# Seven block products in place of eight for part of gate and up in a two-layer decoder trunk

## The reference

```python
h2 = _rmsnorm(x, ffn_norm[l])
ff = jax.nn.silu(jnp.einsum('bsd,df->bsf', h2, w_gate[l])) * jnp.einsum('bsd,df->bsf', h2, w_up[l])
x = x + jnp.einsum('bsf,fd->bsd', ff, w_down[l])
```

## Time and profile before

| what | us |
| --- | --- |
| median of 3 runs | 2231.94 (2230.34 to 2232.48) |
| the profiled execution, its own time | 2232.38 |
| its span | 2230.6 |
| TensorE busy | 2212.5 |
| VectorE busy | 1277.2 |
| ScalarE busy | 948.6 |
| GpSimd busy | 24.0 |
| one pass of the feed-forward loop | 66.2 |

### The profile page before, as it was taken

One profiled execution on the slowest core, in us unless ns is written; L12 is line 12 of the kernel. 1 busy time (PEld: TensorE's weight loads), 2 busy tenths in 40 slices (PEclk: granted clock), 3 DMA queues, 4 the chain that ended last, 5 costly groups with the idle time before them and its releaser, 6 DMA issues.

```text
span 2230.6 us, 27421 instructions
## 1 busy us (share of the span) xinstructions
PE 2212.5 (99%) x11060; PEld 1889.3 (85%) x11060; DVE 1277.2 (57%) x1372; ACT 948.6 (43%) x964; POOL 24.0 (1%) x24
## 2 busy tenths in 40 slices
PE   9999999999999999999999999999999999999998
PEld 7899988888888888888888999888888888888886
DVE  5576774555455555555655866745555455555555
ACT  5554544533333333333443635444333333333333
POOL 0000000000000000000000000000000000000000
PEclk9999999999999999999999999999999999999999
DMA  7543455555555555555555435555555555555554
GB/s 249 183 134 117 157 170 189 182 191 192 189 188 188 188 190 190 192 190 192 193 179 160 147 114 166 174 171 189 197 190 192 190 189 188 188 190 189 192 191 160
DMA packets 221094, 402.67 MB, mean 181 GB/s; under 512 B 13376, under 2 KB 53600, under 8 KB 220896
## 3 DMA queue, kind: packets, MB, share of 16 engines
q1 hardware_dynamic: 220304, 400.90, 54.9%
q10 hardware_dynamic: 720, 0.78, 0.1%
HBM read 399.54 MB, written 2.10 MB: 180 GB/s over the span
## 4 chain that ended last, share of the span: by engine, by line
PE 97%; DMA 1%; DVE 1%; issue 1%; ACT 0%; SPq 0%; POOLq 0%; POOL 0%; ACTq 0%; DVEq 0%
PE bank L631 29%; PE bank L633 29%; PE bank L632 29%; PE bank L591 2%; DMA stage<-in_w_in 1%; PE bank L756 1%; PE bank L985 0%; PE bank L983 0%; PE bank L984 0%; PE bank L697 0%; PE bank L820 0%; PE bank L808 0%; PE bank L698 0%; PE bank L699 0%; PE bank L707 0%
## 5 line engine op out<-in xcount | busy, mean ns | idle before, releaser
L1332 DVE TENSOR_TENSOR w_lo<-stage,w_hi 128x2048 fp32r<-128x2048 f32 (+4 forms) x397 | 859.3, 2166 | 710.5 <-ACT w_hi L1022 710.4
L1022 ACT ACTIVATE w_hi<-stage 128x2048 fp32r<-128x2048 f32 (+4 forms) x397 | 719.8, 1815 | 957.7 <-DMA stage<-in_w_down 308.7
L631 PE MATMUL bank<-w_hi,xt_hi 128*128 128x512 f32 (+4 forms) x2328 | 876.6, 377 | 6.4 <-DVE xt_lo L1393 4.3
L633 PE MATMUL bank<-w_hi,xt_lo 128*128 128x512 f32 (+4 forms) x2328 | 867.7, 373 | 0.0
L632 PE MATMUL bank<-w_lo,xt_hi 128*128 128x512 f32 (+4 forms) x2328 | 867.0, 372 | 0.0
L631 PEld LDWEIGHTS bank<-w_hi,xt_hi 128*128 128x128 f32 x2328 | 437.7, 188 | 80.0 <-issue 11.8
L633 PEld LDWEIGHTS bank<-w_hi,xt_lo 128*128 128x128 f32 x2328 | 437.5, 188 | 69.0
L632 PEld LDWEIGHTS bank<-w_lo,xt_hi 128*128 128x128 f32 x2328 | 437.9, 188 | 67.8
L631 PE MATMUL bank<-w_hi,f_hi 128*128 128x512 f32 x640 | 249.1, 389 | 0.0
L633 PE MATMUL bank<-w_hi,f_lo 128*128 128x512 f32 x640 | 249.0, 389 | 0.0
L632 PE MATMUL bank<-w_lo,f_hi 128*128 128x512 f32 x640 | 249.0, 389 | 0.0
(11 more groups left out here) (213 smaller groups left out, 1231.9 us busy)
## 6 DMA issues: line engine op xcount, KB each, us to landing
stage<-in_w_gate SPq DMA_DIRECT2D x176, 512.0 KB, 4.3
stage<-in_w_up SPq DMA_DIRECT2D x176, 512.0 KB, 4.4
stage<-in_w_down SPq DMA_DIRECT2D x174, 512.0 KB, 4.4
stage<-in_w_in SPq DMA_DIRECT2D x96, 384.0 KB, 3.7
stage<-in_w_out SPq DMA_DIRECT2D x64, 512.0 KB, 4.4
stage<-in_w_in SPq DMA_DIRECT2D x54, 512.0 KB, 4.6
stage<-in_w_in SPq DMA_DIRECT2D x16, 320.0 KB, 3.4
stage<-in_w_q_b SPq DMA_DIRECT2D x12, 384.0 KB, 3.6
```

Of the source, the lines that this page charges most:

```text
L631: pe.matmul(acc, a, wh[:, i, :], start=first and i == 0, stop=False)
L633: mm = pe.matmul(acc, b, wh[:, i, :], start=False, stop=last and i == len(kts) - 1)
L1022: act.activation(w_hi[s][:, 0:kts * cols], stage[s][:, 0:kts * cols], ACT.Copy).then_inc(hi_made[s], 1)
L1332: vec.tensor_tensor(w_lo[s][:, 0:kts * cols], stage[s][:, 0:kts * cols], w_hi[s][:, 0:kts * cols].bitcast(F32), ALU.subtract).then_inc(lo_ ...
```

## The change

In chunks 2 to 10 the first 6 of the 16 row tiles are computed by a scheme of Strassen's kind (Winograd's form). Two token tiles, row tiles q and q+3, and the columns of gate and up form 2x2 blocks. The plain way takes 8 block products; here 7 products of sums of blocks (four sums of token blocks, made once a layer; three sums of weight blocks besides one overwritten block, made for each unit) do, and are combined afterwards. Three units (0, 2 and 4 of a chunk: "sets") hold one such set each, the five others (1, 3, 5, 6, 7: "pairs") hold two row tiles of gate and two of up and are computed plainly. Chunks 0 and 1 stay as they were; chunk 1 now stands ahead of the loop, with the down projection of chunk 0 behind it. The loop runs over chunks 2 to 9. All eight banks are used within a chunk: 0 to 3 for what belongs to one result each, 4 to 7 for products that several results share. `ff_turn` moves from inside gate and up to behind the down units, into banks 4 and 6.

PE (`product` is the three matmuls of a block):

```diff
+SETS = (0, 2, 4)
+PAIRS = (1, 3, 5, 6, 7)
+DOWN_BANKS = (4, 6), (5, 7), (4, 6), (5, 7)
+TURN_BANKS = (4, 6), (0, 1)
...
+                def set_unit(n, q, f, turn):
...
+                    if first:
+                        pe.wait_ge(act_made, layer * (FF_CHUNKS * NT) + NT * f)
+                        pe.wait_ge(xs_made, layer + 1)
+                    product(0, token(0, q), raw[0], first, False)
+                    product(1, mixed_x[3], raw[2], first, False)
+                    product(2, token(1, q), summed[2], first, False)
+                    if first:
+                        added(f - 2, 8)
+                    product(7, mixed_x[0], summed[1], first, last)
+                    product(5, mixed_x[2], summed[0], first, last)
+                    if first:
+                        hidden_in(f - 1)
+                    product(4, token(0, q + K_SET), raw[1], first, last)
+                    product(6, mixed_x[1], raw[3], first, last).then_inc(used[s], 1)
...
                     if c == 0:
-                        for b in (6, 7):
-                            pe.wait_ge(bank_free[b], ROUND[layer, ("ff_turn", 0)][b] + f + 2)
-                        added(f - 1, 6)
-                    elif c == 2:
-                        added(f, 2)
+                        hidden_in(f)
+                        if after_set:
+                            pe.wait_ge(first_kept, layer * SET_CHUNKS + f + 2 - FIRST_SET)
+                            pe.wait_ge(combined, layer * (2 * SET_CHUNKS) + 2 * (f + 1 - FIRST_SET) + 1)
+                    elif c == 1:
+                        if after_set:
+                            pe.wait_ge(combined, layer * (2 * SET_CHUNKS) + 2 * (f + 1 - FIRST_SET) + 2)
                     else:
-                        pe.wait_ge(silu_made if c == 1 else act_made, layer * (FF_CHUNKS * NT) + NT * (f + 2))
+                        added(f, 2 * c - 2)
...
+                with pe.Fori(FIRST_SET, FF_CHUNKS - 1) as f:
+                    gate_up_sets(f, U_BODY, 3 * f - 3 * FIRST_SET)
                     for c in range(4):
-                        down(f - 1, c, U_BODY + 8, 3 * f - 3)
+                        down(f - 1, c, U_BODY + 8, 3 * f - 3 * FIRST_SET)
+                    added(f - 1, 6)
+                    ff_turn(f, TURN_BANKS[0])
```

ACT, preparing a set unit, and DVE, preparing it and in its order around the down units:

```diff
+                    act.activation(w_hi[s][:, 0:3 * NCH], stage[s][:, 0:3 * NCH], ACT.Copy).then_inc(raw_hi_made, 1)
+                    if between:
+                        between()
+                    act.wait_ge(sums_made, layer * (K_SET * SET_CHUNKS) + set_index(n) + 1 + sets)
+                    act.activation(w_hi[s][:, 3 * NCH:], stage[s][:, 3 * NCH:], ACT.Copy)
+                    act.activation(sums_hi[s // 2][:, :, :], sums[s // 2][:, :, :], ACT.Copy).then_inc(hi_made[s], 1)
...
+                    vec.wait_ge(full[s], made(quad, n) * 32)
+                    vec.tensor_tensor(x[:, 0:2, :], w[:, 1:3, :], w[:, 3:4, :].to_broadcast([P, 2, NCH]), ALU.add)\
+                       .then_inc(sum_chain, 1)
+                    vec.wait_ge(sum_chain, 2 * k + 1)
+                    vec.tensor_tensor(w[:, 3, :], x[:, 0, :], w[:, 2, :], ALU.add).then_inc(sum_chain, 1)
+                    vec.wait_ge(sum_chain, 2 * k + 2)
+                    vec.tensor_tensor(x[:, 2, :], w[:, 3, :], w[:, 0, :], ALU.add).then_inc(sums_made, 1)
+                    if between:
+                        between()
+                    vec.wait_ge(sums_made, k + 1)
+                    vec.wait_ge(raw_hi_made, k + 1)
+                    vec.tensor_tensor(w_lo[s][:, 0:3 * NCH], stage[s][:, 0:3 * NCH], w_hi[s][:, 0:3 * NCH].bitcast(F32),
+                                      ALU.subtract)
+                    vec.wait_ge(hi_made[s], made(quad, n))
+                    vec.tensor_tensor(w_lo[s][:, 3 * NCH:], stage[s][:, 3 * NCH:], w_hi[s][:, 3 * NCH:].bitcast(F32),
+                                      ALU.subtract)
+                    vec.tensor_tensor(sums_lo[s // 2][:, :, :], x[:, :, :], sums_hi[s // 2][:, :, :].bitcast(F32),
+                                      ALU.subtract).then_inc(lo_made[s], 1)
...
+                def activate(f, n0, turn):
...
+                    vec.wait_ge(used[3], layer * QUADS + (n0 + 7) // 4 + 2 + turn)
+                    vec.wait_ge(combined, 2 * k + 2)
+                    vec.tensor_tensor(kept[0][:, :], bank[0][:, :], kept[0][:, :], ALU.add).then_inc(gate_made, 1)
+                    vec.tensor_tensor(kept[2][:, :], bank[2][:, :], kept[2][:, :], ALU.subtract).then_inc(gate_made, 1)
+                    vec.tensor_tensor(kept[3][:, :], bank[1][:, :], kept[3][:, :], ALU.add)
+                    vec.tensor_tensor(kept[4][:, :], bank[3][:, :], kept[4][:, :], ALU.add).then_inc(up_made, 1)
+                    vec.wait_ge(up_made, k + 1)
...
+                def down(f, n0, turn=0, sets=0, after_set=True):
+
+                    def between():
+                        add_down(3, n0, turn)
+                        ff_turn(f + 1, TURN_BANKS[0], 0)
+
+                    for c in range(4):
+                        if c == 0 and after_set:
+                            activate(f + 1, n0 - 8, turn)
+                        if c:
+                            add_down(c - 1, n0, turn)
+                        prepare(n0 + c + LEAD, turn, sets, between if c == 3 else None)
```

More of the change, by code:

```diff
@@ L644, in acc_taken @@
                         if layer:
-                            need(x_added, X_ADDS, NT * (2 + parity))
+                            need(x_added, X_ADDS, NT * (3 + parity))
                         return
@@ new lines, in blocks, with product, token @@
+                def blocks(x, n=4):
+                    return x[:, :].rearrange("p (b n) -> p b n", b=n)
+                def product(b, x, w, start, stop):
+                    pe.matmul(bank[b][:, :], x[0], w[0], start=start, stop=False)
+                    pe.matmul(bank[b][:, :], x[0], w[1], start=False, stop=False)
+                    return pe.matmul(bank[b][:, :], x[1], w[0], start=False, stop=stop)
+                def token(t, kt):
+                    return tuple(x[:, kt, t * P:(t + 1) * P] for x in (xt_hi, xt_lo))
@@ new lines, in set_unit @@
+                def set_unit(n, q, f, turn):
+                    s = n % 4
+                    pe.wait_ge(lo_made[s], made(layer * QUADS + n // 4, n) + turn)
+                    raw = [(blocks(w_hi[s])[:, b, :], blocks(w_lo[s])[:, b, :]) for b in range(4)]
+                    summed = [(sums_hi[s // 2][:, b, :], sums_lo[s // 2][:, b, :]) for b in range(3)]
+                    mixed_x = [(xs_hi[:, b, q, :], xs_lo[:, b, q, :]) for b in range(4)]
+                    first, last = q == 0, q == K_SET - 1
+                    if first:
[12 more added lines that the diff above has]
+                    product(6, mixed_x[1], raw[3], first, last).then_inc(used[s], 1)
@@ new lines, in pair_unit @@
+                def pair_unit(n, m, turn):
+                    s = n % 4
+                    pe.wait_ge(lo_made[s], made(layer * QUADS + n // 4, n) + turn)
+                    last = m == len(PAIRS) - 1
+                    for i in range(2):
+                        for t in range(NT):
+                            for part in range(2):
+                                mm = product(2 * t + part, token(t, 2 * K_SET + 2 * m + i),
+                                             (blocks(w_hi[s])[:, 2 * part + i, :], blocks(w_lo[s])[:, 2 * part + i, :]),
+                                             2 * t + part == 3 and m + i == 0, last and i == 1)
+                    mm.then_inc(used[s], 1)
@@ L1254, in gate_up @@
                                    .then_inc(silu_made, 1)
-                gate_up(0, U_FF)
[L1257 to L1262, removed]
+                        if i == 5 and n0 == U_FF:
+                            act.wait_ge(xs_raw, layer + 1)
+                            act.activation(xs_hi[:, :, :, :], xs[:, :, :, :], ACT.Copy).then_inc(xs_hi_made, 1)
@@ new lines, in gate_up_sets, with silus @@
+                def gate_up_sets(f, n0, turn=0, sets=0):
+                    for i in range(8):
+                        if i == SETS[-1] + 1:
+                            act.wait_ge(used[SETS[-1] % 4], layer * QUADS + (n0 + SETS[-1]) // 4 + 2 + turn)
+                            act.activation(kept[0][:, :], bank[4][:, :], ACT.Copy).then_inc(first_kept, 1)
+                        prepare(n0 + i + LEAD, turn, sets)
+                def silus(f):
+                    for t in range(NT):
+                        act.wait_ge(gate_made, layer * (SET_CHUNKS * NT) + NT * (f - FIRST_SET) + t + 1)
+                        act.activation(act_sb[:, t, :], kept[2 * t][:, :], ACT.Silu, scale=rstd_x[:, t:t + 1])\
+                           .then_inc(silu_made, 1)
@@ new lines, in down @@
+                def down(f, n0, turn=0, sets=0, after_set=True):
+                    for c in range(4):
+                        if c == 0 and after_set:
```

(31 more changed lines are left out.)

234 lines of the change are left out of this document (168 added, 66 removed).

## The result

The median is 2272.2 us (2271.1 to 2274.6, four runs) against 2231.3 us: ratio 1.0185, 95% interval 1.0167 to 1.0202. The forecast was 2266, in 2240 to 2290. The profiled execution took 2274.6 us, its span is 2272.7, against 2230.6 before: +42.1.

What follows compares the result with a forecast made beforehand. TensorE was taken to bound the kernel, with VectorE's late adds now stopping it: 2232.4 - 36.7 for matmuls + 56.2 + 5.8 for waits (net +25.3) + 9 for clock falls = 2266.7, 2266 on the median; range 2240 to 2290.

Steps and rivals of the forecast that it cites:

- What it removes: Gate and up, chunks 2 to 10 of both layers: 9 matmuls, 2.04 us, less per changed chunk; -36.7 us.
- VectorE's walk: VectorE's queue followed through the new loop against due times: late adds hold PE 0.78 and 2.73 us a pass.
- T: Start of a pass's first down unit, U8, when the banks of gate and up are complete; 740.85 before the change.
- U10: Third down unit of a pass: waits for U8's adds in banks 4 and 6; PE late 0.78 us.
- U8: First down unit of a pass: its two adds on VectorE end at T+11.66.
- U9: Second down unit: its adds come only after the next pass's first set is prepared, at T+19.83.
- U11: Last down unit of a pass: waits for U9's adds in banks 5 and 7; PE late 2.73 us.
- six falls at 1.5 us: Granted clock falling after a third of the 18 stops of 2.73 us: +9 us.
- the end at which all 18 fall: Rival and upper clock case: every long gap drops the clock, 29 us, 2286; 0.15 of the forecast's chance.
- The prediction's own range: Waits of 3.0 to 4.1 us a pass and 0 to 18 clock falls: 2249 to 2290.
- PE would stay the only bound: Faster rival: the matmul saving arrives in full, 2195; needs SBUF adds at twice the subtracts' rate; chance 0.13.
- The register-valued waits: DVE-bound rival: 0.1 us each, some 15 in the chain, late places grow to 5 us a pass; 2293, chance 0.06.

Runs made afterwards that it cites:

- the reordered kernel: Against the changed kernel, VectorE makes all down units' adds and the hidden-tile copies ahead of the preparation at the same step: 2197.5 us, ratio 0.9849.
- the filled stop: Against the changed kernel, ten useless matmuls added ahead of TensorE's wait at the last down unit, in the passes and chunk 1: 2260.8 us, ratio 1.0135.

## Why the prediction was right

- *What it removes.* 162 matmuls less in the trace; the spacing stayed 0.2267. That they are worth about 36.7 us the reordered kernel shows: the two feed-forward blocks are 17.9 and 16.9 us shorter there (715.4 and 715.5 us from the block's first transpose to its last down matmul, before 733.3 and 732.4).
- *VectorE's walk.* With T = 751.53 in the pass shown (U10's due time 762.41 less 10.88), the adds of U8 were forecast to end at T+11.66 and ended at T+11.67, those of U9 at T+19.83 and T+19.89. Its prices held, the 6.97 us of a set too (763.12 to 770.14 is 7.02), and its operations on PSUM were no dearer than those in SBUF (0.68 us at L1982, 0.69 at L1914). The prediction counts ten on PSUM in the late chain, for an estimate that the sum left aside; the trace has eight.
- *PE's waits.* U10 0.84 on average over 16 passes, forecast 0.78; U11 2.57, forecast 2.73. Chunk 1: 2.88 and 2.94, forecast 2.9, but all at U11. The difference at U11 is mostly that a stop also costs at its end, so that U10 takes longer and U11 is due later: the second matmul starts 0.33 us after the first, not 0.23 (763.33 to 763.66, 771.47 to 771.81). That term was missing, 0.1 a stop; with it a pass is 66.20 - 2.04 + 0.84 + 2.57 + 0.22 = 67.79, and 67.79 is what the pass shown takes; the eight passes without a fall average 67.87.
- *The clock.* I took six falls at 1.5 us. The profiled execution has eight (granted clock 0.992 over the span), in two chunks 1 and six passes. The three others have no trace; from their granted clock, 0.994 and 0.995, I estimate four to six. Passes with a fall average 69.34 us, those without 67.87: 1.47. That the stops cause them was an assumption from one row of the opening; the filled stop has shown it. How many stops would be followed by a fall no row could tell, so that six was near is in part luck; the end at which all 18 fall, 2286, is out. The opening itself falls only in some executions: before the same matmul PE stops for 3.1 us in the kernel with four sets too, and the clock stays at 1.00, where the earlier trace rows had 0.50:

```profile
17.84 0.47 PE L678 MATMUL bank<-w_hi,xt_hi 128*128 128x512 f32 x1 [2.98 <-DVE xt_lo L1548]
...
18.00:20.00 2.00, 2.00 (x10) 1.62 (x10) 1.19 (x3) 1.91 (x4) 0.00 (x0) 1.00 1.06 381
```

- *The sum.* -36.7 + 16 x 3.63 + 2 x 3.0 + 8 x 1.5 = +39.4 of +42.1; the mixers of layer 1 and the opening of the profiled run account for 1.1, 1.6 remains inside the feed-forward blocks. Of that, 1.3 are the 0.08 by which a pass without a fall is longer on average than the sum above; why is not traced. The forecast had +34.3. Of the 7.8 that it lacked, two more falls are 3.0, the waits with their restarts 2.1 (58.1 + 6.0 against 56.2 + 5.8), the rest 2.7. The prediction's own range is summed wrong at its upper end: 4.1 us a pass and 18 falls make 2232.4 - 36.7 + 65.6 + 5.8 + 29 = 2296, not 2290.
- *The rivals.* That PE would stay the only bound is false for this kernel, and true of the same operations in another order. I had priced only a shorter chain as the way to the full gain, adds at twice the rate; another order of the same chain gives it at no cost. The register-valued waits cost nothing: the chain ended within 0.06 us of the forecast. The cause that the prediction named, VectorE reaching the adds behind a set's preparation, is the one shown.

## What to carry to other kernels

An engine with a fifth of its time free (VectorE, 52.6 us of work in a pass of 67.8) can still stop the bound engine: walk its in-order queue against the due times, and put every operation that another engine waits for soon ahead of the long preparations that are due later. Moving one of them alone hands the wait to the next (here from U11 to the transposes, or from U10 to U11); the whole row has to be put in order of due times. And price a stop of TensorE of 2.6 us or more above its length, since the clock may fall behind it.

## What the runs showed of the hardware that I had not expected

- A stop costs TensorE 0.10 to 0.11 us beyond its length at the restart, whether it was 0.25 us long, 0.8 or 2.6: the spacing after the first matmul is 0.33 to 0.34 us in place of 0.23. Where the clock is at 0.50 it is 0.59 in place of 0.43.
- Stops of 0.5 to 1.1 us cost no clock (53 of them in the kernel with the adds of U9 earlier, and no fall there between 21 and 2232 us), nor did one of 1.7 us in the changed kernel's mixers. Of the changed kernel's 16 stops of 2.6 us six were followed by a fall, and both of its stops of 2.9 us; the granted clock of its runs differs (0.992 to 0.995). Of the 18 stops of 3.0 to 3.8 us in the kernel with the adds of U8 earlier 16 were, and half of those falls cost 2.7 us in place of 1.5. The Trainium skill (TensorE: Matmul & The Clock Gate, "Why this matters for your kernels") warns of idle gaps between bursts of matmuls, longer ones than 2.6 us; the trace agrees that gaps cost the clock, and shows that one of 2.6 us can.
- A VectorE addition with a stride-0 (broadcast) operand in SBUF costs what a plain one does: the sums of 1024 take 1.21 us, the subtracts of 1024 before took 1.22.
